# The first map's row minimum in two parts, in the attention of a two-block kernel

## The chip, the cores and the metric

The program runs on 1 core of one Trainium2 chip. The metric is the device time of one execution in microseconds. TensorE (PE) multiplies matrices, VectorE (DVE) and ScalarE (ACT) work element by element, GpSimd (POOL) helps, SyncE (SP) issues weight transfers.

## The reference

The reference is a chain of transformer blocks in float32 on 512 tokens of width 1024, with 256 context tokens in the first part. The change lies in one mixer of it, the differential attention: 8 heads, two maps for each head, 512 queries, 768 keys (512 latent, 256 context), head width 64.

```
def attend(q, k, v):
    s = jnp.einsum('cbhqd,cbhkd->cbhqk', q, k).astype(f32)     # c: the two maps
    p = jax.nn.softmax(s, axis=-1)
    a = p[0] - lam_val * p[1]
    return jnp.einsum('bhqk,bhkv->bhqv', a, v.astype(f32))
k_all = jnp.concatenate([kl, kc], axis=3)     # 512 + 256 keys
v_all = jnp.concatenate([vl, vc], axis=2)
```

The result is normalised over each head's 128 columns and goes through an output projection. Other mixers, gated MLPs and norms come before and after; they are not touched.

## The kernel before, in words

Each engine has a program of its own, written out by hand, and the engines meet through semaphores only. Nothing is scheduled: the order in the loops is the order on the engine. `K.at(...)` names the value at which another engine has done something, `sig(...)` what an instruction announces when it ends. Every VectorE instruction first waits for the one ahead of it on its own engine (`self.wait_ge(self.sem, self.n)`, lines 288 to 311); some wait for another engine as well.

The attention stage works on 32 units, one for each head `h` and block `qt` of 128 queries (`DA_UNITS`). It runs in 35 rounds (`DA_ROUNDS`), as a pipeline: in round i, unit i is scored and its minima and exponentials taken, the maps of unit i-1 are combined, unit i-2 is transposed, unit i-3 is multiplied with the values.

- TensorE (`pe_da_units`): waits for the exponentials that free two of the three score buffers; then the wide scores (512 columns) of map 0 and of map 1, then the narrow ones (256 columns) of map 0 and of map 1. Map 0 uses rows 0 to 63 of the array and map 1 rows 64 to 127. The queries carry a negative scale, so that the softmax takes the row minimum. Only the narrow matmuls announce anything (`da_s`). Then six products of unit i-3 (128 columns each, line 256), then six transposes of unit i-2 (line 265); the last two of these wait for ScalarE's copy of the product.
- VectorE (`dve_da_units`): the minimum over 768 columns of map 0 (line 303); then for unit i-1 a reciprocal (311), a small factor and a 768-column update (299), which combine both maps; then the minimum of map 1 (303). At the end of rounds 8, 12, ..., 32 a square (289) and a sum (303) over 512 columns, for the norm of a finished head.
- ScalarE (`act_da_units`): the exponential of map 0 (389), the scaled copy of the product of unit i-3 (393), the copy of the transposed map of unit i-2 (393), the exponential of map 1 (389). Each exponential waits for its minimum (`da_min`).

A score buffer spans two banks of PSUM: the wide part is in the first, the narrow part in the second. L256, L265, L289, L299, L303, L311, L389 and L393 are the helpers through which these operations go, and other stages use them too, so that a stretch of time or a shape tells the attention's from the others.

Of the kernel before, what the change touches and what calls it, by code (L numbers as in the profile page):

```python
# [15 lines left out]
MUL, ADD, SUB, MAX, MIN = ALU.mult, ALU.add, ALU.subtract, ALU.max, ALU.min  # L16
# [2373 lines left out]
def da_mem(K):  # L2390
    QT = K.mem(WK, 4096).rearrange("p (k n) -> p k n", n=512)
    KT = K.mem(WK + 4096, 6144).rearrange("p (k n) -> p k n", n=768)
    VT = K.mem(WK + 10240, 6144).rearrange("p (t n) -> p t n", n=1024)
    return QT, KT, VT
# [128 lines left out]
def lam_cols(K):  # L2523
    return K.tmpc[:, 100:110]
# [11 lines left out]
def da_unit_mem(K, n):  # L2536

    o = (DW + n % 6 * 1536, CO + C_ONE)[n % 6 == 5]
    e0, e1 = K.mem(o, 768), K.mem(o + 768, 768)
    sc = K.tmpc[:, n % 6 * 8:n % 6 * 8 + 8]  # L2540
    return e0, e1, sc[:, 0:2], sc[:, 2:4], sc[:, 4:6], sc[:, 6:7]


def da_scores(K, n, c):
    i = (2 * n + c) % 3
    return K.psum[:, i * 1024:i * 1024 + 768]


def da_turned(K):
    return K.psum[:, 3072:3840]  # L2550


def da_product(K):
    return K.psum[:, 3840:3968]
# [7 lines left out]
def da_unit(n):  # L2562
    return DA_UNITS[n] if 0 <= n < len(DA_UNITS) else None


def pe_da_units(p, K):
    QT, KT, VT = da_mem(K)
    for i in DA_ROUNDS:
        if da_unit(i):
            h, qt = da_unit(i)  # L2570
            for c in range(2):
                prior = divmod(2 * i + c - 3, 2)
                if prior[0] >= 0:
                    p.wait_ge(*K.at("da_e", *prior))
            for o, size in ((0, 512), (512, 256)):
                for c in range(2):
                    ins = p.mm(da_scores(K, i, c)[:, o:o + size], QT[c * 64:c * 64 + 64, h, qt * 128:(qt + 1) * 128],
                               KT[c * 64:c * 64 + 64, h, o:o + size])
                    if o:
                        ins.then_inc(*p.sig(("da_s", i, c)))  # L2580
        if da_unit(i - 3):
            h, qt = da_unit(i - 3)
            e1 = da_unit_mem(K, i - 3)[1]
            p.wait_ge(*K.at("da_aT", i - 3))
            for c in range(6):
                ins = p.mm(da_product(K), e1[:, c * 128:(c + 1) * 128], VT[:, c, h * 128:(h + 1) * 128], c == 0, c == 5)
            ins.then_inc(*p.sig(("da_o", i - 3)))
        if da_unit(i - 2):
            e0 = da_unit_mem(K, i - 2)[0]
            p.wait_ge(*K.at("da_a", i - 2))  # L2590
            for c in range(6):
                if c == 4 and i >= 3:
                    p.wait_ge(*K.at("da_out", i - 3))
                ins = p.tr(da_turned(K)[:, c * 128:(c + 1) * 128], e0[:, c * 128:(c + 1) * 128])
            ins.then_inc(*p.sig(("da_T", i - 2)))


def act_da_exp(a, K, n, c):
    e, (bias, total) = da_unit_mem(K, n)[c], da_unit_mem(K, n)[2:4]
    if n >= 6:  # L2600
        a.wait_ge(*K.at("da_o", n - 6))
    a.wait_ge(*K.at("da_min", n, c))
    a.act(e, da_scores(K, n, c), ACT.Exp, bias=bias[:, c:c + 1], scale=-1.0, accum_out=total[:, c:c + 1]).then_inc(
        *a.sig(("da_e", n, c)))
# [18 lines left out]
def dve_da_units(v, K):  # L2623
    nlam = lam_cols(K)[:, 2:3]
    for i in DA_ROUNDS:
        for c in range(2):
            if da_unit(i):
                v.wait_ge(*K.at("da_s", i, c))
                v.red(da_unit_mem(K, i)[2][:, c:c + 1], da_scores(K, i, c), MIN).then_inc(*v.sig(("da_min", i, c)))
            if c == 0 and da_unit(i - 1):  # L2630
                e0, e1, bias, total, inv, factor = da_unit_mem(K, i - 1)
                v.wait_ge(*K.at("da_e", i - 1, 1))
                v.rcp(inv, total).then_inc(*v.sig())
                v.stt(factor, total[:, 0:1], nlam, inv[:, 1:2], MUL, MUL).then_inc(*v.sig())
                v.stt(e0, e1, factor, e0, MUL, ADD).then_inc(*v.sig(("da_a", i - 1)))
        if i >= 8 and i % 4 == 0:
            dve_da_square(v, K, i // 4 - 2)
# [21 lines left out]
def dve_da_square(v, K, h):  # L2659
    sq, O = K.mem(CO + 1664, 512), K.mem(WK + h * 512, 512)  # L2660
    v.wait_ge(*K.at("da_out", 4 * h + 3))
    v.tt(sq, O, O, MUL).then_inc(*v.sig())
    v.red(da_sums(K, h), r2(sq, 4), ADD).then_inc(*v.sig(("da_sq", h)))
# [1848 lines left out]
def pe_program(p, K):  # L4512
# [25 lines left out]
    pe_da_proj(p, K, t3)  # L4538
    p.meet("da_proj")
    pe_da_units(p, K)  # L4540
    pe_out(p, K, "da_out", K.I["da_w_out"][0], 8, 4, ("daT_lo",), turn=pe_da_turn(p, K))
    yield "ln3"
# [95 lines left out]
def dve_program(v, K):  # L4638
# [33 lines left out]
    dve_da_proj(v, K, t3)  # L4672
    v.meet("da_proj")
    dve_da_units(v, K)
    dve_da_tail(v, K)
    v.wait_ge(*K.at("gate_rows", 1, 0))
# [173 lines left out]
```

## Time and profile before

| | |
|---|---|
| time, median of 3 runs | 4184.85 us (4183.09 to 4189.86) |
| the profiled execution | 4193.0 us, span 4191.2 us |
| busy, whole span | PE 3883.7, PEld 3189.0, DVE 2150.9, ACT 1665.2, POOL 617.2 us |
| attention units | about 1758 to 1915 us of the span |
| busy in 1758 to 1915 | PE 127.00, PEld 87.01, DVE 116.65, ACT 101.47, POOL 0.00 us |

Times in the profile are from the start of the span, in microseconds unless ns is written. A busy time says how long an engine worked, not that it set the end: for that the chain of waits is read, which goes back from the last instruction, at each step to what released it. Matmuls are pipelined, so that rows of them overlap. "DVEq" is the queue of VectorE, which spends an instruction of its own where an instruction waits for two semaphores.

### The profile page before, as it was taken

The numbers are of one execution on the slowest core, as the hardware profiler recorded it, in microseconds if no ns is written. First come the engines' busy times: TensorE is split into PE (matmuls) and PEld (weight loads), VectorE is DVE, ScalarE is ACT, GpSimd is POOL, SyncE is SP. The second block draws the span as 40 slices with busy tenths as digits, with TensorE's granted clock in tenths as the row PEclk, the third lists the DMA queues.
The fourth block names the chain that finished last, engine by engine and source line by source line (L and its number), as shares of the span: only waits on it lengthen the run. The fifth ranks groups of instructions, "written<-read, shape, count | busy, mean of one in ns | idle before, by whom it ended". The sixth has DMA issues, their size and how long they took to land.

```text
span 4191.2 us, 67651 instructions
## 1 busy us (share of the span) xinstructions
PE 3883.7 (93%) x28266; PEld 3189.0 (76%) x28266; DVE 2150.9 (51%) x3078; ACT 1665.2 (40%) x2708; POOL 617.2 (15%) x676
## 2 busy tenths in 40 slices
PE   6999999788999988987899899999999998899999
PEld 4877777677888866756788675778888878778887
DVE  3667754753222453377323654555665428655564
ACT  4445454322112242263323346554334335544333
POOL 0045554422000001003000000000210003000120
PEclk8999999798999999999999899999999999999999
DMA  4254553221121121103222320231323230312332
GB/s 162 89 170 147 159 167 125 70 89 61 61 70 51 61 87 51 50 1 112 81 94 93 71 81 11 73 101 62 101 94 106 90 111 3 130 65 81 101 101 81
DMA packets 235991, 367.67 MB, mean 88 GB/s; under 512 B 9811, under 2 KB 142630, under 8 KB 235302
## 3 DMA queue, kind: packets, MB, share of 16 engines
q1 hardware_dynamic: 217200, 300.49, 21.9%
q0 software_dynamic: 17936, 62.70, 4.8%
q8 instruction: 222, 3.64, 0.4%
q14 instruction: 83, 0.68, 0.1%
q10 hardware_dynamic: 550, 0.17, 0.0%
HBM read 344.36 MB, written 18.96 MB: 87 GB/s over the span
## 4 chain that ended last, share of the span: by engine, by line
PE 76%; DVE 13%; ACT 7%; issue 1%; DMA 1%; ACTq 0%; POOL 0%; DVEq 0%; SPq 0%; POOLq 0%
PE psum L259 21%; PE psum L260 20%; PE psum L261 20%; PE psum L256 13%; DVE arena L289 3%; ACT arena L389 3%; PE psum L265 2%; DVE arena L299 2%; DVE rw L289 2%; DVE rx L383 2%; ACT arena L393 1%; DVE arena L303 1%; ACT rw L393 1%; ACT rx L393 1%; DVE arena L315 1%
## 5 line engine op out<-in xcount | busy, mean ns | idle before, releaser
L259 PE MATMUL psum<-rx,rw 128*128 128x512 f32 (+2 forms) x2864 | 1056.9, 369 | 55.2 <-DVE rx L383 29.3
L260 PE MATMUL psum<-rx,rw 128*128 128x512 f32 (+2 forms) x2864 | 1030.8, 360 | 0.0
L261 PE MATMUL psum<-rx,rw 128*128 128x512 f32 (+2 forms) x2864 | 1029.4, 359 | 0.0
L289 DVE TENSOR_TENSOR rw<-arena,rw 128x2048 fp32r<-128x2048 f32 (+3 forms) x266 | 546.5, 2054 | 811.7 <-ACT rw L393 802.1
L256 PE MATMUL psum<-arena 32*32 32x32 f32 (+11 forms) x12982 | 767.9, 248 | 120.3 <-ACT arena L393 48.0
L256 PEld LDWEIGHTS psum<-arena 32*32 32x32 f32 (+5 forms) x12982 | 586.2, 134 | 260.2 <-issue 83.7
L393 ACT ACTIVATE rw<-arena 128x2048 fp32r<-128x2048 f32 (+3 forms) x266 | 453.6, 1705 | 754.5 <-PE psum L261 739.6
L259 PE MATMUL psum<-rw,rx 128*128 128x512 f32 (+1 forms) x1720 | 682.0, 396 | 31.1 <-DVE rx L383 13.8
L259 PEld LDWEIGHTS psum<-rx,rw 128*128 128x128 f32 (+1 forms) x2864 | 550.5, 192 | 191.9 <-DVE rx L383 42.7
L260 PE MATMUL psum<-rw,rx 128*128 128x512 f32 (+1 forms) x1720 | 673.4, 392 | 0.0
L261 PE MATMUL psum<-rw,rx 128*128 128x512 f32 (+1 forms) x1720 | 673.1, 391 | 0.0
L260 PEld LDWEIGHTS psum<-rx,rw 128*128 128x128 f32 (+1 forms) x2864 | 551.9, 193 | 79.4 <-issue 4.1
L261 PEld LDWEIGHTS psum<-rx,rw 128*128 128x128 f32 (+1 forms) x2864 | 550.5, 192 | 79.5
L393 ACT ACTIVATE arena<-psum 128x512 f32<-128x512 f32 (+6 forms) x675 | 313.9, 465 | 742.1 <-PE psum L261 360.1
L454 POOL TENSOR_TENSOR arena<-arena 128x512 f32<-128x512 f32 (+5 forms) x300 | 436.0, 1453 | 960.6 <-DVE arena L299 389.3
L259 PEld LDWEIGHTS psum<-rw,rx 128*128 128x128 f32 x1720 | 327.8, 191 | 112.3 <-DVE rx L383 25.7
L389 ACT ACTIVATE arena<-arena 128x512 f32<-128x512 f32 (+11 forms) x481 | 250.6, 521 | 401.5 <-DVE arena L299 164.7
L299 DVE SCALAR_TENSOR_TENSOR arena<-arena 128x512 f32<-128x512 f32 (+8 forms) x481 | 374.7, 779 | 30.2 <-ACT arena L389 13.3
L261 PEld LDWEIGHTS psum<-rw,rx 128*128 128x128 f32 x1720 | 327.3, 190 | 68.1
L260 PEld LDWEIGHTS psum<-rw,rx 128*128 128x128 f32 x1720 | 327.9, 191 | 64.3
L289 DVE TENSOR_TENSOR arena<-arena,psum 128x512 f32<-128x512 f32 (+3 forms) x308 | 151.8, 493 | 370.6 <-PE psum L261 204.5
L265 PE MATMUL psum<-arena 128*128 128x128 f32 (+1 forms) x1284 | 196.2, 291 | 90.2 <-DVE arena L289 22.1
(73 smaller groups left out, 2204.4 us busy)
## 6 DMA issues: line engine op xcount, KB each, us to landing
arena<-in_ffn_w_up SPq DMA_DIRECT2D x66, 1024.0 KB, 5.1
arena<-in_ada_w SPq DMA_DIRECT2D x48, 1024.0 KB, 6.1
arena<-in_ffn_w_down SPq DMA_DIRECT2D x40, 1024.0 KB, 4.9
arena<-in_ffn_w_gate SPq DMA_DIRECT2D x22, 1024.0 KB, 5.1
arena<-in_dn_w_in SPq DMA_DIRECT2D x16, 1024.0 KB, 5.8
arena<-in_xa_w_kv SPq DMA_DIRECT2D x16, 1024.0 KB, 5.0
arena<-in_hgrn_w_in SPq DMA_DIRECT2D x16, 1024.0 KB, 5.4
arena<-in_da_w_in SPq DMA_DIRECT2D x12, 1024.0 KB, 5.1
```

The lines of the kernel that those rows point to most:

```text
L256: return self.e.matmul(out, l, r, start=start, stop=stop)
L259: self.e.matmul(out, l[0], r[0], start=start, stop=False)
L260: self.e.matmul(out, l[0], r[1], start=False, stop=False)
L261: return self.e.matmul(out, l[1], r[0], start=False, stop=stop)
L265: return self.e.transpose(out, a, self.K.ident[0:k, 0:k])
L289: return self.e.tensor_tensor(out, a, b, op)
L299: return self.e.scalar_tensor_tensor(out=out, in0=a, scalar=s, in1=b, op0=op0, op1=op1)
L303: return self.e.tensor_reduce(out, a, AX.X, op)
L383: return self.e.tensor_tensor(dst[1], src, dst[0].bitcast(F32), SUB)
L389: return self.e.activation(out, a, f, **kw)
L393: return self.e.activation(out, a, ACT.Copy, **kw)
L454: return self.e.tensor_tensor(out, a, b, op)
```

## The change

The first wide matmul of each round now announces its end (`da_wide`). VectorE takes the minimum of map 0 in three instructions: over the 512 wide columns, which waits for `da_wide`; over the 256 narrow columns, which waits for `da_s` as the single one did; and the lesser of the two, a 128x1 operation, whose end is now `da_min` of map 0. A free column of the unit's small block holds the second value. The minimum of map 1 and all else stays.

```
--- before.py
+++ after.py
@@ -2538,7 +2538,7 @@
     o = (DW + n % 6 * 1536, CO + C_ONE)[n % 6 == 5]
     e0, e1 = K.mem(o, 768), K.mem(o + 768, 768)
     sc = K.tmpc[:, n % 6 * 8:n % 6 * 8 + 8]
-    return e0, e1, sc[:, 0:2], sc[:, 2:4], sc[:, 4:6], sc[:, 6:7]
+    return e0, e1, sc[:, 0:2], sc[:, 2:4], sc[:, 4:6], sc[:, 6:7], sc[:, 7:8]
 
 
 def da_scores(K, n, c):
@@ -2578,6 +2578,8 @@
                                KT[c * 64:c * 64 + 64, h, o:o + size])
                     if o:
                         ins.then_inc(*p.sig(("da_s", i, c)))
+                    elif c == 0:
+                        ins.then_inc(*p.sig(("da_wide", i)))
         if da_unit(i - 3):
             h, qt = da_unit(i - 3)
             e1 = da_unit_mem(K, i - 3)[1]
@@ -2624,11 +2626,18 @@
     nlam = lam_cols(K)[:, 2:3]
     for i in DA_ROUNDS:
         for c in range(2):
-            if da_unit(i):
-                v.wait_ge(*K.at("da_s", i, c))
-                v.red(da_unit_mem(K, i)[2][:, c:c + 1], da_scores(K, i, c), MIN).then_inc(*v.sig(("da_min", i, c)))
+            if da_unit(i) and c == 0:
+                least, other = da_unit_mem(K, i)[2][:, 0:1], da_unit_mem(K, i)[6]
+                v.wait_ge(*K.at("da_wide", i))
+                v.red(least, da_scores(K, i, 0)[:, 0:512], MIN).then_inc(*v.sig())
+                v.wait_ge(*K.at("da_s", i, 0))
+                v.red(other, da_scores(K, i, 0)[:, 512:768], MIN).then_inc(*v.sig())
+                v.tt(least, least, other, MIN).then_inc(*v.sig(("da_min", i, 0)))
+            elif da_unit(i):
+                v.wait_ge(*K.at("da_s", i, 1))
+                v.red(da_unit_mem(K, i)[2][:, 1:2], da_scores(K, i, 1), MIN).then_inc(*v.sig(("da_min", i, 1)))
             if c == 0 and da_unit(i - 1):
-                e0, e1, bias, total, inv, factor = da_unit_mem(K, i - 1)
+                e0, e1, bias, total, inv, factor, other = da_unit_mem(K, i - 1)
                 v.wait_ge(*K.at("da_e", i - 1, 1))
                 v.rcp(inv, total).then_inc(*v.sig())
                 v.stt(factor, total[:, 0:1], nlam, inv[:, 1:2], MUL, MUL).then_inc(*v.sig())
```

TensorE's instructions are the same in number and order. On VectorE, the round with the first square and the first minimum of the next round, before (arena is SBUF, psum the scores; the 128x512 operation is the square, the 128x4 one its sum):

```order
L299 SCALAR_TENSOR_TENSOR arena<-arena 128x768 [waits s_dve]
L303 TENSOR_REDUCE arena<-psum 128x1 [waits s_dve,s_pe]
L289 TENSOR_TENSOR arena<-arena 128x512 [waits s_dve]
L303 TENSOR_REDUCE arena<-arena 128x4 [waits s_dve]
L303 TENSOR_REDUCE arena<-psum 128x1 [waits s_dve,s_pe]
L311 RECIPROCAL arena<-arena 128x2 [waits s_dve,s_act]
```

The same place now:

```order
L299 SCALAR_TENSOR_TENSOR arena<-arena 128x768 [waits s_dve]
L303 TENSOR_REDUCE arena<-psum 128x1 [waits s_dve,s_pe]
L289 TENSOR_TENSOR arena<-arena 128x512 [waits s_dve]
L303 TENSOR_REDUCE arena<-arena 128x4 [waits s_dve]
L303 TENSOR_REDUCE arena<-psum 128x1 [waits s_dve,s_pe] x2
L289 TENSOR_TENSOR arena<-arena 128x1 [waits s_dve]
L311 RECIPROCAL arena<-arena 128x2 [waits s_dve,s_act]
```

The first minimum has become two reductions and a 128x1 operation between the sum and the reciprocal. In an ordinary round, where the second minimum of one round and the first of the next are neighbours, before:

```order
L299 SCALAR_TENSOR_TENSOR arena<-arena 128x768 [waits s_dve]
L303 TENSOR_REDUCE arena<-psum 128x1 [waits s_dve,s_pe] x2
L311 RECIPROCAL arena<-arena 128x2 [waits s_dve,s_act]
L299 SCALAR_TENSOR_TENSOR arena<-arena 128x1 [waits s_dve]
L299 SCALAR_TENSOR_TENSOR arena<-arena 128x768 [waits s_dve]
```

The same place now:

```order
L299 SCALAR_TENSOR_TENSOR arena<-arena 128x768 [waits s_dve]
L303 TENSOR_REDUCE arena<-psum 128x1 [waits s_dve,s_pe] x3
L289 TENSOR_TENSOR arena<-arena 128x1 [waits s_dve]
L311 RECIPROCAL arena<-arena 128x2 [waits s_dve,s_act]
L299 SCALAR_TENSOR_TENSOR arena<-arena 128x1 [waits s_dve]
L299 SCALAR_TENSOR_TENSOR arena<-arena 128x768 [waits s_dve]
```

Of the three reductions in a row the first is the previous round's second minimum; the other two are the halves of the first, and both wait for two semaphores. Nothing else has moved.

## Rows read from the trace of the kernel before

**Rows 1.** The page: the span, and the shares of the chain that ended last.

```profile
span 4191.2 us, 67651 instructions
...
PE 76%; DVE 13%; ACT 7%; issue 1%; DMA 1%; ACTq 0%; POOL 0%; DVEq 0%; SPq 0%; POOLq 0%
```

**Rows 2.** The chain of waits in the attention stage (1758 to 1916 us).

```profile
by line: PE psum L256 28.7%; DVE arena L303 26.1%; ACT arena L389 16.6%; PE psum L265 7.5%; ACT arena L393 7.3%; DVE arena L299 5.6%; issue 3.8%; DVE arena L289 3.2%; DVE arena L311 0.8%; ACTq L195 0.3%; DVEq L195 0.3%; DVE arena L294 0.1%
```

**Rows 3.** The chain through one ordinary round (1802 to 1807 us): start, us, what.

```profile
1803.05 0.44 PE psum L265 x2
1803.49 1.54 PE psum L256 x8
1805.03 0.95 DVE arena L303
1806.01 1.00 ACT arena L389 x2
```

**Rows 4.** The chain around a round with squares (1795 to 1803 us).

```profile
1798.05 0.97 DVE arena L303
...
1799.04 0.70 DVE arena L289
...
1799.77 0.70 DVE arena L303
...
1800.49 0.02 DVEq L195
...
1800.56 0.97 DVE arena L303
```

**Rows 5.** Timeline of VectorE, an ordinary round: start, us, operation [idle <-releaser].

```profile
1826.17 0.96 DVE L303 TENSOR_REDUCE arena<-psum 128x1 f32<-128x768 f32 x1
...
1827.98 0.96 DVE L303 TENSOR_REDUCE arena<-psum 128x1 f32<-128x768 f32 x1 [0.86 <-PE psum L256]
```

**Rows 6.** VectorE groups over the whole span, by shape: count | busy, mean ns.

```profile
L303 DVE TENSOR_REDUCE arena<-psum 128x1 f32<-128x768 f32 x64 | 61.3, 958 | 27.9 <-PE psum L256 23.8
L303 DVE TENSOR_REDUCE arena<-psum 128x2 f32<-128x512 f32 x28 | 19.4, 692 | 45.8 <-PE psum L256 45.2
L303 DVE TENSOR_REDUCE arena<-psum 128x2 f32<-128x256 f32 x4 | 1.7, 424 | 5.2 <-PE psum L256 5.0
L289 DVE TENSOR_TENSOR arena<-arena 128x1 f32<-128x1 f32 x1 | 0.2, 160 | 0.3 <-ACT arena L389 0.3
```

**Rows 7.** TensorE, last passes of wide and narrow scores, in two rounds: start, us.

```profile
1812.87 0.60 PE L256 MATMUL psum<-arena 64*128 64x512 f32 x2
1813.51 0.38 PE L256 MATMUL psum<-arena 64*128 64x256 f32 x2
1763.76 1.06 PE L256 MATMUL psum<-arena 64*128 64x512 f32 x2
1765.04 0.63 PE L256 MATMUL psum<-arena 64*128 64x256 f32 x2
```

**Rows 8.** The windows of both clock levels: stretch, busy of each engine, PEclk.

```profile
1762.70:1765.70 3.00, 2.93 (x8) 1.18 (x8) 0.00 (x0) 0.99 (x2) 0.00 (x0) 0.50 0.00 0
1767.80:1904.00 136.20, 115.10 (x766) 79.43 (x766) 107.72 (x163) 93.22 (x177) 0.00 (x0) 1.00 0.00 1
```

**Rows 9.** Timeline of VectorE: the first rounds, and the last one behind squares.

```profile
1765.70 0.96 DVE L303 TENSOR_REDUCE arena<-psum 128x1 f32<-128x768 f32 x1 [3.14 <-PE psum L256]
...
1768.34 2.02 DVE L303 TENSOR_REDUCE arena<-psum 128x1 f32<-128x768 f32 x2
...
1772.04 2.03 DVE L303 TENSOR_REDUCE arena<-psum 128x1 f32<-128x768 f32 x2
...
1893.14 0.96 DVE L303 TENSOR_REDUCE arena<-psum 128x1 f32<-128x768 f32 x1
```

**Rows 10.** TensorE at the end of the projections: start, us.

```profile
1750.61 0.39 PE L261 MATMUL psum<-rw,rx 128*128 128x512 f32 x1
1750.84 0.39 PE L259 MATMUL psum<-rw,rx 128*128 128x512 f32 x1
```

## The prediction

> **What bounds the kernel now.** I read the page first: 76% of the chain that ended last is TensorE, and VectorE has 13% [rows 1]. The change touches one stage of 158 us, so I then followed the chain of waits inside it. There the shares are quite other: the row minima (L303) alone hold 26.1% of that chain, the matmuls of scores and products (L256) 28.7%, and the exponentials (L389) 16.6% [rows 2]. So the minimum is on the path, and what it takes counts.
>
> The pieces of one ordinary round show the ring [rows 3]: last two transposes 0.44, scores 1.54, minimum of the first map 0.95, its exponential 1.00, then the scaled copy of the product 0.38 and the transposes again. From the first minimum at 1800.56 to the next at 1805.03 it is 4.47 us [rows 3, 4]. The minimum of the second map starts 1.81 us before the next round's first minimum and VectorE is then idle for 0.86 us, waiting for TensorE [rows 5]. In a round with squares it is another engine that is late: minimum, square and sum follow each other without idle time, and the next first minimum starts behind them at 1800.56 [rows 4], not when its scores are there. Six first minima stand so, behind a pair of squares (h = 0 to 5, in rounds 8, 12 to 28), the last of them at 1893.14 [rows 9]. The first minima of rounds 2 and 3 also start directly behind a second minimum: both are in the pairs of 2.02 and 2.03 us [rows 9].
>
> **The durations.** A minimum of 768 columns in PSUM takes 0.958 us, one of 512 takes 0.692, one of 256 takes 0.424 (both in two groups a row, otherwise the same operation), and a 128x1 operation of two tensors 0.160 [rows 6]. The three minima lie on one line (266 ns for 256 columns, then 268), so I take 0.692 and 0.424 as they stand. Between VectorE instructions there are two gaps. Behind a minimum, the square, which waits for its own engine alone, starts 0.03 us after its predecessor's end (1798.05 + 0.958 to 1799.04). The minimum behind the sum waits for TensorE too, which costs the queue an instruction of its own (the 0.02 piece of DVEq); it starts 0.10 us behind the end (1799.77 + 0.69 to 1800.56) [rows 4]. The narrow minimum is of the second kind, the combining minimum of the first.
>
> So one first minimum now costs VectorE 0.692 + 0.10 + 0.424 + 0.03 + 0.160 = 1.41 us where it cost 0.958: 0.45 us more.
>
> **What the earlier start gives.** The scores of the two maps run side by side: the last wide passes of both stand in one row of two that is 0.60 us long. The wide part's last pass starts at 1812.87 and ends at 1813.47, the narrow part's ends at 1813.51 + 0.38 = 1813.89 [rows 7]. The wide part is thus done only 0.42 us ahead. TensorE's granted clock was 1.00 there and in the whole of 1767.8 to 1904 [rows 8]; at 0.50, its lower level of 1.2 GHz, the same distance is 1765.67 - 1764.82 = 0.85 us [rows 7, 8].
>
> Ordinary rounds: the wide minimum may start 0.42 us earlier, and the idle 0.86 us [rows 5] gives room for it. The result is late by 0.45 - 0.42 = 0.03 us. There are 32 first minima; less rounds 0 and 1, rounds 2 and 3, and the six behind squares, 22 are left: 22 x 0.03 = +0.7 us.
>
> Rounds behind squares: VectorE comes free long after the scores, so nothing starts earlier and the whole 0.45 is on the path: 6 x 0.45 = +2.7 us.
>
> Rounds 2 and 3: likewise, 2 x 0.45 = +0.9 us. In round 2 ScalarE is nearly as late as the minimum, which could take off a tenth.
>
> Rounds 0 and 1 run at the lower level, at least in part. There the wide minimum is through (0.692 + 0.10 = 0.79) before the narrow scores are, 0.85 later. What follows the scores is then 0.04 + 0.424 + 0.03 + 0.16 = 0.65 instead of 0.04 + 0.958 = 1.00: 2 x 0.35 = -0.7 us.
>
> Sum: 0.7 + 2.7 + 0.9 - 0.7 = **+3.6 us**. No DMA is moved, no wait is put on TensorE or ScalarE. Behind the waiting wide minimum in VectorE's queue are the narrow one, the combination, the reciprocal, the two updates of the previous unit and the second minimum; they stood behind the same kind of wait before, and measured from the combination's end their times stay. The second exponential and the transposes follow them unchanged. Everything after the stage starts later by the sum, since its chain begins with what the last round leaves.
>
> **Costs that the trace doesn't show.** First, the new signal on the first wide matmul. Nearest rows: at the end of each group of 24 products in the projections the last matmul (L261) carries a signal and the next (L259) starts 0.23 us later, as between all others [rows 10]: cost 0. From the other side: if the signal kept the next pass waiting until the wide pass has ended, that is 0.60 - 0.43 = 0.17 us a round (the pass takes 0.60, and the passes behind it start in step with the columns: 0.64 us for the 768 from 1812.87 to 1813.51, so 0.43 for 512 [rows 7]), 32 x 0.17 = 5.4 us. I take 0, the nearest row. A gain is excluded, a signal takes no work away.
> *TensorE: Matmul & The Clock Gate*, section "The cost: per-tile semaphore tail", of the Trainium skill holds that signals of matmuls that run side by side come one after the other, about 26 ns each. An estimate by that page is 32 x 0.026 = 0.8 us on top, a sum of 4.4; no row here shows such a tail.
>
> Second, the gap between wide and narrow. It is 0.10 by [rows 4]; were the wait for TensorE, met long ago, free, it would be 0.03, and with all 32 rounds 0.07 cheaper the sum is 3.6 - 2.2 = 1.4 us. I take 0.10, since both waits of the minimum at 1800.56 were for things done before its predecessor ended too.
> *VectorE: DVE Perf Modes*, section "The DRAIN you can't avoid", of the Trainium skill says that operations chained with a semaphore after each took as long as without. By that rule the sum would be the 1.4; the trace speaks against it for an instruction with two waits (0.10 against 0.03).
>
> **The rivals.**
> (a) *The narrow remainder is all that is left after the scores*, as the words of the change have it: each of the 24 rounds that wait for TensorE gains 0.35, -8.4, and the eight others cost 3.6: -4.8 us. For it: rounds at the lower level. Against it: at the higher one the wide minimum needs 0.79 us and has 0.42. It would take a stage at the lower level throughout, and even so stays within what counts as no change.
> (b) *The signal parts the score matmuls*: +3.6 + 5.4 = +9.0 us, slower than before by 0.21%. The place is the wide pass of each round, the price 0.17 us. It decides from (8.4 - 3.6) / 32 = 0.15 us a round. For it: such a signal in the middle of a run of 64-row passes stands nowhere in the trace. Against it: [rows 10].
> (c) *The gaps are cheap*: +1.4 us, above.
> (d) *VectorE's idle time behind the second minimum isn't there in ordinary rounds*, and the 0.45 falls due in all of the 30 later rounds: 30 x 0.45 - 0.7 = +12.8 us. Against it: the 0.86 idle is twice the 0.42 needed.
>
> **The numbers.** The profiled execution took 4193.0 us (span 4191.2), 8.15 over the median 4184.85 of the three runs; with the sum it would be 4196.6. For the median I add to the median: 4184.85 + 3.6 = 4188.4. Chances: forecast 0.66, (c) 0.20, (a) 0.04, (b) 0.06, (d) 0.04. The bounds of the unknown costs give +1.4 to +9.0, so 4186.2 to 4193.9; the runs before lie 1.8 below and 5.0 above their median, and a median of a few runs can be off by about 3: I say 4183 to 4194.5. 0.2% of this kernel, about what its measurement can tell from no change, is 8.4 us. Forecast, (a) and (c) are within it; (b) and (d) beyond, and scatter can carry the forecast over. Faster 0.02, same 0.90, slower 0.08.
>
> **What the profile would show.** Wide minima of 0.69, narrow ones of 0.42 and 32 combining operations of 0.16; 64 more VectorE instructions, and some 32 x 0.32 = 10 us more of its busy time. In ordinary rounds the idle time before the wide minimum is 0.86 - 0.42 = 0.44 and the period 4.50; from the second minimum in a square round to the exponential behind it 0.45 more; wide passes 0.43 behind each other as before. The stage, 1758.56 to the last round, is longer by 3 to 4 us. It is wrong if the ordinary period shrinks (a, c), if the score passes move apart (b), or if the idle time before the wide minimum is gone in ordinary rounds (d).

## The result, and the profile after

The changed kernel is slower, by a little that is clear of noise. Its median over 10 runs is 4198.8 us (4194.12 to 4207.27), that of the kernel before over 10 runs 4190.84 us; the ratio is 1.0023, 95% interval 1.0015 to 1.0031, that is +9.6 us (6.3 to 13.0). A second comparison on another occasion gave 1.0020 (1.0010 to 1.0029). The forecast was 4188.4 us, no change by its bound, in a range of 4183 to 4194.5. Of the 10.4 us between forecast and result, 6.0 are the base: the three runs shown ahead had a median of 4184.85, ten runs 4190.84. The other 4.4 are the change's effect, 8.0 between the two medians where 3.6 were worked out; by the ratio even 6.0.

The two profiled executions differ by 14.3 us in their spans (4205.5 against 4191.2), and less than that is the change. I measured the stage by itself: from the start of the last VectorE instruction ahead of the scores (L294) to the exponential of map 0 in round 31, the last round that scores a unit. Both ends are rows of the timeline (start, us, operation [idle before <- what ended it]). Before:

```profile
1758.35 0.15 DVE L294 TENSOR_SCALAR arena<-arena 128x1 f32<-128x1 f32 x1
...
1903.04 0.90 ACT L389 ACTIVATE arena<-psum,arena 128x768 f32<-128x768 f32 x1 [0.58 <-DVE arena L303]
```

After:

```profile
1762.46 0.15 DVE L294 TENSOR_SCALAR arena<-arena 128x1 f32<-128x1 f32 x1
...
1915.00 0.90 ACT L389 ACTIVATE arena<-psum,arena 128x768 f32<-128x768 f32 x1 [0.60 <-DVE arena L289]
```

That is 144.7 us before and 152.5 after: **+7.8 us**. The stage already started 4.1 us later, before any changed instruction. In the fourteen profiles of this study that start lies anywhere from 1747 to 1763 us and what follows the stage varies by 4 us, without regard to the version, so the stage's length is the measure to use. It is read from one execution each. Where VectorE did the same work twice, the two lengths agree to 0.1 us: 144.7 and 144.8 (kernel before, experiment 1), 152.5 and 152.5 (changed kernel), 144.2 and 144.2 (experiment 7).

The VectorE groups of the changed kernel, by shape (count | busy, mean ns | idle), answer to [rows 6]. Of the 33 operations in the last row 32 are the combining minima:

```profile
L303 DVE TENSOR_REDUCE arena<-psum 128x1 f32<-128x768 f32 x32 | 30.7, 958 | 3.3
L303 DVE TENSOR_REDUCE arena<-psum 128x1 f32<-128x512 f32 x32 | 22.1, 692 | 17.3 <-PE psum L256 16.7
...
L303 DVE TENSOR_REDUCE arena<-psum 128x1 f32<-128x256 f32 x32 | 13.6, 425 | 3.6 <-PE psum L256 1.0
L289 DVE TENSOR_TENSOR arena<-arena 128x1 f32<-128x1 f32 x33 | 5.3, 160 | 1.4 <-ACT arena L389 0.3
```

An ordinary round, answering to [rows 5]:

```profile
1790.92 0.96 DVE L303 TENSOR_REDUCE arena<-psum 128x1 f32<-128x768 f32 x1
1792.31 1.22 DVE L303 TENSOR_REDUCE arena<-psum 128x1 f32<-128x512 f32 x2 [0.43 <-PE psum L256]
1793.56 0.16 DVE L289 TENSOR_TENSOR arena<-arena 128x1 f32<-128x1 f32 x1
```

The pair of 1.22 us is 0.692 + 0.425 and a gap of 0.10; before the wide minimum VectorE is still idle for 0.43. And the first round behind squares, answering to [rows 4]:

```profile
1804.72 0.96 DVE L303 TENSOR_REDUCE arena<-psum 128x1 f32<-128x768 f32 x1
1805.71 0.69 DVE L289 TENSOR_TENSOR arena<-arena 128x512 f32<-128x512 f32 x1
1806.44 0.69 DVE L303 TENSOR_REDUCE arena<-arena 128x4 f32<-128x512 f32 x1
1807.23 1.22 DVE L303 TENSOR_REDUCE arena<-psum 128x1 f32<-128x512 f32 x2
1808.48 0.16 DVE L289 TENSOR_TENSOR arena<-arena 128x1 f32<-128x1 f32 x1
```

All this is as forecast. What was not is in the windows (stretch, length, busy time and count of PE, PEld, DVE, ACT and POOL, then PEclk, DMA share, GB/s). They cover the same two stretches from the stage's start on. Before:

```profile
1758.50:1766.40 7.90, 4.90 (x16) 1.96 (x16) 2.61 (x4) 1.98 (x4) 0.00 (x0) 0.57 0.00 0
1766.40:1775.60 9.20, 5.90 (x38) 3.99 (x38) 8.25 (x14) 6.14 (x12) 0.00 (x0) 1.00 0.01 2
```

After:

```profile
1762.60:1770.50 7.90, 5.00 (x16) 2.02 (x16) 3.69 (x9) 2.25 (x5) 0.00 (x0) 0.56 0.00 0
1770.50:1779.70 9.20, 8.01 (x25) 4.43 (x26) 7.11 (x13) 4.53 (x10) 0.00 (x0) 0.50 0.01 2
...
1811.40:1814.80 3.40, 3.40 (x16) 2.50 (x13) 2.54 (x6) 2.06 (x5) 0.00 (x0) 0.50 0.00 0
```

Before, TensorE is back at 2.4 GHz (PEclk 1.00) after some 7 us of the stage at 1.2; after, it stays at 1.2 GHz for some 17. And in the middle, where the kernel before has 1.00 throughout [rows 8], the clock fell twice for about 3.4 us, the first time at 1811.4.

### The profile page after: what moved, and what is told of

It is laid out like the page before. It is cut to its first block, busy times and chain, and to the rows that moved or that the text cites. A ratio compares the mean times of both kernels' runs of the same rounds, so it can differ in the third digit from the quotient of the medians.

```text
span 4205.5 us, 67747 instructions
## 1 busy us (share of the span) xinstructions
PE 3898.1 (93%) x28266; PEld 3198.2 (76%) x28266; DVE 2163.6 (51%) x3142; ACT 1666.1 (40%) x2708; POOL 617.1 (15%) x676
## 4 chain that ended last, share of the span: by engine, by line
PE 77%; DVE 13%; ACT 7%; issue 1%; DMA 1%; ACTq 0%; DVEq 0%; POOL 0%; SPq 0%; POOLq 0%
PE psum L259 21%; PE psum L260 20%; PE psum L261 20%; PE psum L256 13%; DVE arena L289 3%; ACT arena L389 3%; PE psum L265 2%; DVE arena L299 2%; DVE rw L289 2%; DVE rx L383 2%; DVE arena L303 1%; ACT arena L393 1%; ACT rw L393 1%; ACT rx L393 1%; DVE arena L315 1%
```

## The account of the stage

I took the distance from one round's exponential of map 0 to the next round's from the profiles. After against before:

| part | before | after | difference |
|---|---|---|---|
| start to exponential of round 4 | 20.23 | 22.32 | +2.09 |
| 21 ordinary distances, the four with a fall of the clock taken at 4.48 | 4.455 | 4.48 | 21 x 0.025 = +0.5 |
| six distances into a round behind squares | 5.15 | 5.60 | 6 x 0.456 = +2.7 |
| two falls of the clock | 2 x 4.48, twice | 4.72 + 5.30, 4.89 + 5.13 | +2.1 |
| one stall of VectorE, round 8 | 5.60 | 5.96 | +0.36 |
| sum | 144.7 | 152.5 | +7.8 |

The second and third line are the prediction's. The experiments ask where the first and fourth come from. In the expectations "sum" is the theory that only instruction times, gaps and waits count; "clock" is the theory that TensorE's changed pattern of work and waits alters the granted clock, which then costs time of its own. Each was a variant of the changed kernel unless it says otherwise.

## Experiments 1 to 4: the parts of the change

**1. The signal alone.** The first wide matmul still announces its end, VectorE's split is off.

```
-            if da_unit(i) and c == 0:
+            if da_unit(i) and c == 0 and False:
             ...
             elif da_unit(i):
-                v.wait_ge(*K.at("da_s", i, 1))
-                v.red(da_unit_mem(K, i)[2][:, 1:2], da_scores(K, i, 1), MIN).then_inc(*v.sig(("da_min", i, 1)))
+                v.wait_ge(*K.at("da_s", i, c))
+                v.red(da_unit_mem(K, i)[2][:, c:c + 1], da_scores(K, i, c), MIN).then_inc(*v.sig(("da_min", i, c)))
```

The second part, which takes either map's minimum unsplit, stands in experiments 2 to 4, 6 to 8 and 11 too; there only the condition is given.

> The first wide matmul of each round announces its end, and nobody waits for it; VectorE takes the minimum over 768 columns as before. If only VectorE's work and TensorE's waits count, the time is that of the kernel before within 2 us and the stage's ordinary period 4.46 us. If the signal parts the score matmuls (0.17 us a round), it is 5.4 us slower and the two maps' passes start more than 10 ns apart.

Ratio 0.9999 (0.9991 to 1.0008), stage 144.8 us. Its timeline, an ordinary round:

```profile
1801.29 0.96 DVE L303 TENSOR_REDUCE arena<-psum 128x1 f32<-128x768 f32 x1
1803.11 0.96 DVE L303 TENSOR_REDUCE arena<-psum 128x1 f32<-128x768 f32 x1 [0.86 <-PE psum L256]
...
1807.56 0.96 DVE L303 TENSOR_REDUCE arena<-psum 128x1 f32<-128x768 f32 x1 [0.86 <-PE psum L256]
```

The period is 4.45 us and the idle time 0.86, as before. The signal costs nothing that can be seen; the 5.4 us of rival (b) are out.

**2. Split everywhere but behind squares** (`... and c == 0 and not (i > 8 and i % 4 == 1)`).

> Split in all rounds but the six behind squares. By the sum of instruction times alone: 22 x 0.03 for ordinary rounds and +0.2 for rounds 0 to 3, together about +1 us over the kernel before. By the clock theory: the split in rounds 0 to 3 lengthens the stretch at 1.2 GHz at the stage's start (from about 7 to about 17 us) and costs some 2 us there, so about +3 us; in the middle of the stage no fall of the granted clock, since no round is longer than before.

Ratio 1.0002 (0.9993 to 1.0011), which can't tell 1 from 3 us; the stage can: 147.6, +2.9. Some 17 us at 1.2 GHz at the start again, no fall in the middle. The stall of +0.35 in round 8 is there too.

**3. Split only behind squares** (`... and c == 0 and i > 8 and i % 4 == 1`).

> Split only in the six rounds behind squares, where VectorE is late anyway. By the sum of instruction times: 6 x 0.45 = +2.7 us, periods of 5.60 us where they were 5.15. By the clock theory: the same, and in addition falls of the granted clock in the middle of the stage behind such rounds (there were two in the changed kernel, 1.06 us each), so +3.5 to +6 us; the start of the stage as in the kernel before, some 7 us at 1.2 GHz.

Ratio 1.0006 (0.9998 to 1.0015); stage 148.7, +4.0: 6 x 0.45 = 2.7, one fall in the middle (5.06 + 4.93 in place of 8.92, +1.07), and 0.2 at the start. Low clock at the start for 7 us only.

**4. Split from round 4 on** (`... and c == 0 and i >= 4`).

> Split from round 4 on. By the sum: 22 x 0.03 + 6 x 0.45 = +3.4 us. By the clock theory: the start of the stage is that of the kernel before (some 7 us at 1.2 GHz instead of 17), and behind squares one to three falls of the granted clock, so +4.5 to +6.5 us. If the long start of the changed kernel was chance, it may show here as well.

Ratio 1.0010 (1.0000 to 1.0019); stage 150.2, +5.5, with two falls in the middle and the start of the kernel before (7 us). So the clock at the start goes with the split in rounds 0 to 3, and the falls in the middle with the longer rounds behind squares.

## Experiments 5 to 8: what the clock answers to

**5. The wait without the split.** The kernel before, with a sum over 256 columns ahead of the first minimum of the six rounds behind squares:

```
         for c in range(2):
+            if da_unit(i) and c == 0 and i > 8 and i % 4 == 1:
+                v.red(K.tmpc[:, 47:48], K.mem(CO + 1664, 256), ADD).then_inc(*v.sig())
             if da_unit(i):
                 v.wait_ge(*K.at("da_s", i, c))
```

> The kernel before, with one more VectorE instruction (a sum over 256 columns in SBUF, whose result nobody reads) ahead of the first minimum in the six rounds behind squares: nothing is split, VectorE is only some 0.4 us later there. By the sum +2.4 to +2.8 us. If the falls of the granted clock in the middle of the stage come from TensorE's longer wait alone, one or two appear here, some 1.06 us each: +3.5 to +5 us. If they come from the split, none.

Ratio 1.0005 (0.9996 to 1.0013); stage 148.5, +3.8: six distances of 5.60 and one fall, +1.07 (5.09 + 4.90). TensorE's timeline around it, and the window of the fall:

```profile
1894.42 0.44 PE L265 MATMUL psum<-arena 128*128 128x128 f32 x2 [0.56 <-ACT arena L393]
...
1897.72 0.60 PE L265 MATMUL psum<-arena 128*128 128x128 f32 x4
1900.02 0.44 PE L265 MATMUL psum<-arena 128*128 128x128 f32 x2 [1.70 <-ACT arena L393]
1900.38 4.71 PE L256 MATMUL psum<-arena 64*128 64x512 f32 x20
```

```profile
1901.30:1904.50 3.20, 3.20 (x15) 2.34 (x12) 1.72 (x4) 1.90 (x5) 0.00 (x0) 0.50 0.00 0
```

In an ordinary round TensorE waits 0.56 us ahead of its last two transposes. Here it waited 1.70, and just over a microsecond after its return the clock fell. In the kernel before the same wait is 1.25 us:

```profile
1803.05 0.44 PE L265 MATMUL psum<-arena 128*128 128x128 f32 x2 [1.25 <-ACT arena L393]
```

In the changed kernel it is 1.70 too, and 2.06 at the place of the stall, where the first fall came:

```profile
1810.18 0.44 PE L265 MATMUL psum<-arena 128*128 128x128 f32 x2 [2.06 <-ACT arena L393]
...
1830.28 0.44 PE L265 MATMUL psum<-arena 128*128 128x128 f32 x2 [1.70 <-ACT arena L393]
```

Nothing is split in this version, so a fall doesn't need the split. One fall in one execution is thin by itself; the weight lies in all profiles taken together. The five with six waits of 1.70 or more each (experiments 3, 4, 5 and the changed kernel twice; two of the thirty are the 2.06 at the stall) had 1, 2, 1, 2 and 2 falls in the middle, 8 behind 30 waits, and both waits of 2.06 are among the eight. The nine others had none: 41 waits of 1.25, in experiment 2 one of 1.60 (at the stall), in experiments 10 and 11 none over 1. The wait and the length of the round grow together in all of these, so which of the two the clock answers to isn't told apart. Nor is it known why just these eight waits were followed by a fall.

**6. Split only in rounds 2 and 3** (`... and c == 0 and i in (2, 3)`).

> Split only in rounds 2 and 3, which start behind a second minimum. By the sum the stage is 0.9 us longer: the distances of the exponentials of rounds 1, 2 and 3 go from 3.70 to 4.15. The clock theory has two forms: if the early finish in rounds 0 and 1 keeps the clock down, it comes back after some 7 us here as before; if VectorE's later minima in rounds 2 and 3 do, it stays down for some 17 us.

One execution: stage 145.8, +1.1: 0.43 and 0.46 in the two rounds (4.15 and 4.16 for 3.72 and 3.70), 0.2 at the start. The clock came back after 7 us. The later minima of rounds 2 and 3 do not keep it down.

**7. Split only in rounds 0 and 1** (`... and c == 0 and i < 2`), twice. The first time is one execution.

> Split only in rounds 0 and 1, both at 1.2 GHz, where the first minimum comes about 0.35 us earlier. By the sum of instruction times the stage is 0.7 us shorter. By the clock theory TensorE has done its scores of round 1 earlier and then waits; the granted clock stays at 1.2 GHz for some 17 us as in the changed kernel, rounds 1 to 3 take 4.7 us instead of 3.7, and the stage is 2 us longer.

Stage 144.2, shorter than before by 0.5, and the clock came back after 7 us. The clock theory failed in this form: up to the moment of the return this kernel does what the changed one does. What differed was when the clock had fallen, a little earlier with respect to the first score. So it ran again:

> Split only in rounds 0 and 1 once more. The clock came back after some 7 us the first time, though up to that point its work is that of the changed kernel. If the moment at which the clock fell (1.0 us into the stage instead of 1.1 to 1.2) decides, both are possible here: 17 us and a stage of some 146.5 us when it falls at 1.1 or later, 7 us and 144.2 when it falls at 1.0. If rounds 2 and 3 decide, always 7 us.

Ratio 1.0003 (0.9993 to 1.0012). Stage 144.2 and 7 us again, and it fell early again.

**8. Split only in rounds 0 to 3** (`... and c == 0 and i < 4`).

> Split in rounds 0 to 3 alone. By the sum of instruction times the stage is 0.2 us longer than before. If the early minima of rounds 0 and 1 keep the clock at 1.2 GHz (at least where it falls late), 17 us of it and a stage of some 146.8 us; no fall in the middle, since the rounds there are as before.

One execution: stage 146.8, +2.1; 17 us at 1.2 GHz. The mean granted clock in the first 2 us of scores shows when it fell (lower is earlier). In this order: experiment 7, its repetition, experiment 8:

```profile
1746.80:1748.80 2.00, 2.00 (x8) 0.84 (x8) 0.68 (x1) 0.00 (x0) 0.00 (x0) 0.71 0.00 0
```

```profile
1749.82:1751.82 2.00, 2.00 (x8) 0.84 (x8) 0.64 (x1) 0.00 (x0) 0.00 (x0) 0.70 0.00 0
```

```profile
1754.44:1756.44 2.00, 2.00 (x8) 0.83 (x8) 0.69 (x1) 0.00 (x0) 0.00 (x0) 0.72 0.00 0
```

And the next stretch, 7.90 to 17.10 us from the stage's start, of the repetition and of experiment 8:

```profile
1757.50:1766.70 9.20, 6.17 (x40) 4.19 (x40) 8.18 (x14) 6.14 (x12) 0.00 (x0) 1.00 0.01 2
```

```profile
1762.20:1771.40 9.20, 7.90 (x25) 4.32 (x26) 7.14 (x14) 4.63 (x9) 0.00 (x0) 0.50 0.01 2
```

The table of all profiles, by that mean:

| split in rounds 0 and 1 | mean clock, first 2 us of scores | at 1.2 GHz |
|---|---|---|
| no, 7 profiles | 0.70, 0.70, 0.71, 0.72, 0.75, 0.76, 0.76 | 7 us, all |
| yes, 2 | 0.70, 0.71 | 7 us |
| yes, 5 | 0.72, 0.72, 0.73, 0.74, 0.74 | 17 us, all |

The long start stands only where the first rounds are split, in five of seven such profiles and in none of the seven others. The two exceptions are those with the earliest falls, but the line between them is thin (0.71 and 0.72), so that the moment of the fall is the likely second condition and not a shown one. That rounds 2 and 3 are not needed for it is shown: they come behind the moment at which the clock returned, and experiment 11 below, whose first eight rounds are those of experiment 7, had 17 us. Why is argued, not shown. At 1.2 GHz, and with the clock falling at the same moment, the split brings the exponential of round 0 forward by 0.35 us (3.20 from the stage's start in experiment 7, 3.55 in experiment 6) and shortens the way to that of round 1 by 0.34 (5.00 to 4.66), so TensorE does the same scores earlier and waits longer behind them. How late the clock falls differs between executions, and none of these edits reaches back before it; the two early falls may be luck.

## Experiments 9 to 11: the change again, and a better version

**9. The changed kernel again.**

> The changed kernel once more, against the kernel before on the same chip. By the sum of instruction times +3.6 us (ratio 1.0009). By the clock theory the stage takes some 7 to 8 us more than before (152 us from its start to the last exponential of map 0 instead of 144.7): 17 us at 1.2 GHz at its start if that is not chance, and one to three falls behind squares; ratio 1.0015 to 1.0025.

Ratio 1.0020 (1.0010 to 1.0029), stage 152.5: 17 us at the start, two falls in the middle at the same distances from the start as in the first profile (49 and 107 us), and the stall. Neither was a chance of one execution.

**10. Squares spread, unsplit.** The longest term was the VectorE-bound round, so I took the kernel before and put the square and its sum in two rounds:

```
         if i >= 8 and i % 4 == 0:
-            dve_da_square(v, K, i // 4 - 2)
+            dve_da_square(v, K, i // 4 - 2, (0,))
+        if i >= 8 and i % 4 == 1:
+            dve_da_square(v, K, i // 4 - 2, (1,))
...
+    if 0 in parts:
+        v.wait_ge(*K.at("da_out", 4 * h + 3))
+        v.tt(sq, O, O, MUL).then_inc(*v.sig())
+    if 1 in parts:
+        v.red(da_sums(K, h), r2(sq, 4), ADD).then_inc(*v.sig(("da_sq", h)))
```

> The kernel before, unsplit, with the square at the end of rounds 8, 12, ..., 32 and its sum a round later, at the end of rounds 9, 13, ..., 33. Each (0.69 and 0.03 of gap) fits in the 0.86 us in which VectorE waits for TensorE in an ordinary round, so that no round is longer than 4.46: 6 x 0.69 = -4.1 us against the kernel before, and no fall of the clock in the middle. If the fit is too tight, -2 us or less.

Ratio 0.9990 (0.9981 to 0.9999), stage 140.6, -4.1 as expected. Its timeline:

```profile
1795.86 0.96 DVE L303 TENSOR_REDUCE arena<-psum 128x1 f32<-128x768 f32 x1
1796.85 0.69 DVE L289 TENSOR_TENSOR arena<-arena 128x512 f32<-128x512 f32 x1
1797.68 0.96 DVE L303 TENSOR_REDUCE arena<-psum 128x1 f32<-128x768 f32 x1
...
1801.31 0.69 DVE L303 TENSOR_REDUCE arena<-arena 128x4 f32<-128x512 f32 x1
1802.14 0.96 DVE L303 TENSOR_REDUCE arena<-psum 128x1 f32<-128x768 f32 x1
```

The first minima are 4.46 us apart: each half fits in the idle 0.86. This version's stage is shorter than that of both kernels; its time is below the kernel before by 0.10%, just clear of noise.

**11. The same, with the split in rounds 0 and 1.**

> Squares and sums in separate rounds, and the split in rounds 0 and 1 alone. By the sum -4.1 - 0.7 = -4.8 us against the kernel before, a stage of some 140 us. If the early finish keeps the clock at 1.2 GHz at the start, 2 us of that are lost: -2 to -3 us, and the unsplit version with spread squares is the better one.

Ratio 1.0002 (0.9993 to 1.0011), stage 143.2: 2.6 us worse than experiment 10, of which 2.2 stand ahead of round 4 (22.48 from the start in place of 20.25) and 0.33 are a stall of VectorE in round 25. Its next stretch from the start:

```profile
1765.40:1774.60 9.20, 7.47 (x23) 3.90 (x24) 5.82 (x10) 4.71 (x9) 0.00 (x0) 0.50 0.01 2
```

The clock stayed at 1.2 GHz for 17 us. Rounds 2 and 3, unsplit here, take 5.06 us at that clock; split, in the changed kernel, 4.72. So the split does gain there, 0.34 a round, what rival (a) claimed for the lower clock.

## Why the prediction was wrong

- *One first minimum costs 0.45 more on VectorE.* Right: 0.692, 0.10, 0.425, 0.03, 0.160; six distances behind squares grew by 0.456. The gap of 0.10 held, rival (c) is out.
- *Ordinary rounds +0.03.* Right: 4.48 for 4.455, with 0.43 idle left (0.44 forecast); rival (d) is out. (The period before, 4.47 in the prediction, was read off the chain; the exponentials give 4.455. And (c) took the cheaper gap 32 times, though the sum holds it only 30 times: 1.5 us rather than 1.4.)
- *The signal costs nothing.* Right (experiment 1): 144.8 for 144.7 leaves room neither for the 5.4 us of rival (b) nor for the estimate of 0.8.
- *Rounds 0 to 3: +0.9 - 0.7 = +0.2.* The single terms held where the clock was the same: 0.35 + 0.34 = 0.69 less in rounds 0 and 1 (experiment 7 against 6; against the kernel before, whose clock fell 0.2 us later, it was 0.5), +0.9 in rounds 2 and 3 (6). Their sum did not: split together they took +2.1 (experiments 2, 8, 9). **This is the first step that failed.** I took for granted that TensorE would be at the higher clock from round 2 on, as [rows 8] show it before. In the changed kernel it was at 1.2 GHz until the scores of round 4, and a round takes 4.72 us there and not 3.70 or 4.15.
- *Rounds behind squares cost 0.45 each and nothing else.* The 0.45 was right (0.456), the "nothing else" not. **This is the second step that failed.** It priced TensorE's longer wait as time, but not as a cause: 1.25 us became 1.70, the clock then fell behind two of the six, 1.06 us each. Experiment 5 has such a fall with no split at all.
- *A stall of VectorE, 0.36 us.* It wasn't in the sum. It stands in all three profiles with the split in the first rounds and in the ordinary ones: the reciprocal of round 8 began 0.46 us behind its predecessor in place of 0.10, with no engine to wait for. I counted VectorE's records from L294 on, its queue's included. Wherever such a gap can be seen in this stage, it is at the 91st or the 219th, 128 further on, and about 0.7 us behind it a packet of 8 KB starts on a DMA queue that the profile calls "instruction". The kernel before has the same place, in round 11, and experiment 5 too. The rows are of the changed kernel, the kernel before, experiment 5 (its round 11) and experiment 11, each the gap itself, and last the DMA of 1803.0 to 1804.5 of the changed kernel (packets, MB, share):

```profile
1803.14 0.17 DVE L311 RECIPROCAL arena<-arena 128x2 f32<-128x2 f32 x1 [0.46 <-DVE arena L289]
...
1810.91 1.27 DVE L299 SCALAR_TENSOR_TENSOR arena<-arena 128x1 f32<-128x1 f32 x2 [0.22 <-DVE arena L311]
...
1812.99 0.17 DVE L311 RECIPROCAL arena<-arena 128x2 f32<-128x2 f32 x1 [0.46 <-DVE arena L303]
...
1875.61 0.96 DVE L303 TENSOR_REDUCE arena<-psum 128x1 f32<-128x768 f32 x1 [0.47 <-PE psum L265]
...
q14 instruction: 1, 0.01, 1.8%
```

In an ordinary round it cost nothing, since VectorE has 0.86 us of idle time there: the distance around 1812.99 stayed 4.46. The split's added instructions brought the 91st forward into round 8, where minimum, square and sum leave no idle time; in experiment 11 the 219th falls in the round in which the sum fills it. So adding instructions had a price of its own, the shift of that place. That VectorE waits there for its next instructions to be loaded is argued from the packet and the 128, not shown.
- *The base.* Three runs gave a median 6.0 us below that of ten. The margin of 3 us that I put on a median of a few runs was half of what it had to be; later groups of 21 to 35 runs of the kernel before had medians of 4189.4 to 4190.9.

The two middle terms were forecast at 3.4 and measured 3.3. Of the 7.8 in all, 1.9 at the start (2.1 where 0.2 were forecast) and 2.1 in the two falls came through the clock, about half, and 0.36 through the stall.

## What to carry to other kernels

Splitting a reduction to start it early pays only if the first part is done by the time the second part's data are there, and only where the engine is idle at that time; look for the rounds in which it is the late one, since there the added time is paid in full. Where such rounds are, try to spread their extra work over rounds with idle time: here that took 4.1 us off the stage, and the split added 7.8. In a stage where TensorE waits in every round, price a longer wait twice: as time, and as the chance that its clock falls behind it. And when the effect sought is a thousandth of the whole, measure the stage and not only the program: the ratios of experiments 2 to 5 could not tell the cases apart, the stage's length could.

## What the hardware showed that I had not expected

- TensorE's granted clock fell from 2.4 to 1.2 GHz behind 8 of 30 waits of 1.70 us or more (rounds of 5.60, two of them of 5.96), and behind none of 41 waits of 1.25 (rounds of 5.15) and one of 1.60 (5.50). One such fall cost 1.06 us.
- Finishing earlier can go with a slower stage: at the start, 0.7 us gained over two rounds went, in five of seven executions, with some 10 us more at the lower clock, and the changed kernel's first four rounds took 2.1 us more.
- VectorE lost up to 0.36 us at two places of this stage that lie 128 of its records apart (its queue's counted), each with an 8 KB packet of the instruction queue 0.7 us behind. It cost time only in rounds in which VectorE was the late engine.
- A VectorE instruction that waits for a second semaphore starts 0.10 us behind its predecessor, one that waits for its own engine alone 0.03, though in both cases the waits for other engines are over. *VectorE: DVE Perf Modes*, section "The DRAIN you can't avoid", of the Trainium skill takes a semaphore after each operation as free; for a second one the pairs of 1.22 us speak against it.
